# A norm applied behind its projection, and a gated attention in another order

## The reference, cut to what is touched

```python
# end of the first block, and its gated linear attention (2 pairs of heads, width 64 and 128)
x = x + 0.5 * m_l[8] * swiglu(modulate(rms_norm(x, norm3_w), m_l[6], m_l[7]), ffn2_w1, ffn2_w3, ffn2_w2)
x = rms_norm(x, final_norm_w)
# second block
xn = rmsnorm(h, norm_mix_g)
q, k, v, u, y = split(xn @ w_in, [512, 1024, 1536, 2048])
attn = dilated_mixture_attention(rope(q), rope(k), v)
uc = centred_depthwise_conv(u, conv_w, conv_b)
rec = bidirectional_rglru(uc, ...) * gelu(y)
h = h + concat([attn, rec]) @ w_out
h = h + memory_cross_attention(rmsnorm(h, norm_cross_g), rmsnorm(mem, norm_mem_g), w_cq, w_ck, w_cv, w_co)
```

## Time and profile before

| | us |
|---|---|
| median of three runs | 2144.28 |
| lowest, highest | 2143.29, 2144.73 |
| the execution that was profiled | 2144.28 |
| its span in the profile | 2142.5 |

### The profile page before, as it was taken

The page is one execution under the profiler, slowest core; times in us unless marked ns, Lnnn a source line. Parts: engine busy times, 40 slices in busy tenths (PEclk is TensorE's granted clock), DMA queues, the critical chain, the costliest instruction groups (busy, mean ns, idle before and its releaser), DMA issues.

```text
span 2142.5 us, 26436 instructions
## 1 busy us (share of the span) xinstructions
PE 2000.4 (93%) x9594; PEld 1671.9 (78%) x9594; DVE 913.5 (43%) x1361; ACT 748.5 (35%) x1056; POOL 732.9 (34%) x324
## 2 busy tenths in 40 slices
PE   5999999999989999778899999979988989999997
PEld 2999999999967775455788888857764857888886
DVE  4633377235444404773411212168976444121124
ACT  4321122112337115443342222346646344232231
POOL 1333233323413221242344443524340323443532
PEclk8999999999989999978999999989989999999999
DMA  8332244234312221001223232323140212332321
GB/s 322 120 126 75 83 160 165 78 118 148 117 45 83 60 64 43 20 1 40 93 89 116 80 108 89 109 68 108 60 128 1 89 49 80 108 99 87 108 85 63
DMA packets 53273, 197.20 MB, mean 92 GB/s; under 512 B 6304, under 2 KB 6864, under 8 KB 51408
## 3 DMA queue, kind: packets, MB, share of 16 engines
q1 hardware_dynamic: 44272, 162.98, 23.8%
q10 hardware_dynamic: 8928, 33.23, 4.3%
HBM read 194.09 MB, written 2.10 MB: 92 GB/s over the span
## 4 chain that ended last, share of the span: by engine, by line
PE 62%; issue 19%; DVE 8%; POOL 6%; ACT 3%; DMA 1%; SPq 1%; POOLq 0%; DVEq 0%; ACTq 0%
PE ps L1715 49%; POOL wlo L517 6%; PE ps L1702 1%; PE ps L1703 1%; PE ps L1704 1%; PE ps L2014 1%; DMA ada_f<-ada_p 1%; PE ps L1945 1%; PE ps L1936 1%; DVE s_gla L1434 1%; PE ps L1729 1%; PE ps L2101 1%; PE ps L2085 1%; PE ps L2075 1%; PE ps L2122 1%
## 5 line engine op out<-in xcount | busy, mean ns | idle before, releaser
L517 POOL TENSOR_TENSOR wlo<-raw,whi 128x1024 fp32r<-128x1024 f32 x280 | 692.6, 2486 | 1319.5 <-ACT whi L553 1297.5
L1715 PE MATMUL ps<-h_hi,whi 128*128 128x512 f32 (+2 forms) x1568 | 510.3, 364 | 16.5 <-POOL wlo L517 8.5
L1715 PE MATMUL ps<-h_lo,whi 128*128 128x512 f32 (+2 forms) x1568 | 507.6, 362 | 0.0
L1715 PE MATMUL ps<-h_hi,wlo 128*128 128x512 f32 (+2 forms) x1568 | 506.8, 362 | 0.0
L553 ACT ACTIVATE whi<-raw 128x1024 fp32r<-128x1024 f32 x280 | 289.5, 1053 | 417.5 <-PE ps L1715 339.5
L1715 PEld LDWEIGHTS ps<-h_hi,whi 128*128 128x128 f32 x1568 | 287.8, 189 | 57.6 <-issue 8.5
L1715 PEld LDWEIGHTS ps<-h_lo,whi 128*128 128x128 f32 x1568 | 288.3, 189 | 33.2 <-issue 1.0
L1715 PEld LDWEIGHTS ps<-h_hi,wlo 128*128 128x128 f32 x1568 | 288.2, 189 | 33.4
L1715 PE MATMUL ps<-g_hi,wlo 128*128 128x512 f32 (+1 forms) x784 | 257.3, 364 | 0.0
L1715 PE MATMUL ps<-g_hi,whi 128*128 128x512 f32 (+1 forms) x784 | 257.3, 364 | 0.0
L1715 PE MATMUL ps<-g_lo,whi 128*128 128x512 f32 (+1 forms) x784 | 257.3, 364 | 0.0
(11 more groups left out here) (385 smaller groups left out, 2304.2 us busy)
## 6 DMA issues: line engine op xcount, KB each, us to landing
raw<-panels SPq DMA_DIRECT2D x280, 512.0 KB, 3.5
ada_w<-ada_t ACTq DMA_DIRECT2D x54, 512.0 KB, 4.3
ada_f<-ada_p SPq DMA_DIRECT2D x8, 1024.0 KB, 18.7
x_lat<-x_t SPq DMA_DIRECT2D x1, 2048.0 KB, 7.9
out<-x_lat SPq DMA_DIRECT2D x8, 256.0 KB, 2.2
x_ctx<-ctx_t SPq DMA_DIRECT2D x1, 1024.0 KB, 9.9
cond_b<-cond SPq DMA_DIRECT2D x1, 1024.0 KB, 23.1
ada_x<-ada_t SPq DMA_DIRECT2D x2, 512.0 KB, 21.3
```

What stands on the lines that cost most here:

```text
L517: pool.tensor_tensor(wlo[:, sl], raw[:, sl], whi[:, sl].bitcast(f32), ALU.subtract).then_inc(lo_done, 1)
L1715: ins = pe.matmul(bank(banks + b, n), wt[:, w], a[:, at_(kc, c0):at_(kc, c0) + n], start=kc == 0 and j == 0, stop=kc == n_k - 1 and j == 2)
```

## The change

**Between the blocks.** Norm 4 becomes late. The memory's squares, their sum, the split with its weight (`memory_squares`, `memory_sums`, `memory_hi`, `memory_lo`), the sum over partitions and the root (`memory_stats`, `memory_root`, `memory_inverse`) move between the groups of the feed-forward layer. In the last group each output is scaled by the product of both weights and split (`mix_parts`, `scaled_hi`); the sums come in the middle of the first pair, the transposes behind it (`mix_spread`). 1/rms is applied later: to u and y by VectorE on their way out of PSUM (`scaled_in`), to q and k through the cosines and sines, to v and cv as ScalarE's scale, to ck by VectorE (`memory_keys`). gelu then runs in place on ScalarE. `final_rows`, the block's own norm of `x_lat`, comes behind the first two pieces. The load of `mem` starts before W_out.

**Recurrence.** `RG_STEPS` gives every step its piece; two steps of part 3 stand between the roundings for v.

**Gated attention.** The context's exponentials are made before the last fill piece, into a tile `ctx_x` of their own; VectorE's head 3 steps and ScalarE's last rounding move into the first levels; level 7's masked copy goes to ScalarE (four copies of 64 rows); and the first pair's norm product waits behind all levels of the second, with `spread_copy` taking the factors out of PSUM.

```diff
@@ input_projection2, ScalarE
+                act.wait_ge(mem_ready, 1)
+                act.wait_ge(cs_arg, 1)
...
+                    if kind == "v":
+                        for c, step in enumerate((None, 1, 2, None)):
+                            q = P_WIN2 + first + 3 + c
+                            if step:
+                                rg_step(3, step)
+                            round_panel(q % RING, q // RING + 1, q - RING)
...
+                    if n == 0:
+                        mix_root()
...
                     elif kind == "y":
+                        act.wait_ge(win2_evac, 4 + j + 1)
+                        y = ry[:, j * LAT:(j + 1) * LAT]
+                        act.activation(y, y, ACT.Gelu_apprx_tanh).then_inc(gelu_done, 1)
...
+                    if n in RG_STEPS:
+                        rg_step(*RG_STEPS[n])
@@ hidden_down, VectorE
+                def mix_parts(o):
+                    scaled_lo(norms[4], o)
+                    if o:
+                        add_both(o)
...
                         if o and G["layer"] == 1:
+                            mix_parts(o - 1)
...
+                    if G["layer"] == 1:
+                        mix_parts(KC - 1)
@@ input_projection2, VectorE
+                def scaled_in(n):
+                    dve.wait_ge(panel_done, done(P_WIN2 + n))
+                    dve.wait_ge(lat_rows, 1)
+                    dst = (ru if n < 4 else ry)[:, n % 4 * LAT:(n % 4 + 1) * LAT]
+                    dve.tensor_tensor(dst, bank(2 * (n % RING)), r_lat[:, :], ALU.mult).then_inc(win2_evac, 1)
...
+                scaled_in(0)
+                scaled_in(1)
+                final_rows()
...
+                for c in range(4):
+                    if c >= 2:
+                        scaled_in(c)
+                    rg_convolution(c)
+                dve.wait_ge(rg_conv, 4)
+                scaled_in(4)
+                scaled_in(5)
+                scaled_in(6)
...
                 rg_gated(0)
+                scaled_in(7)
...
                 rotate(6)
+                memory_keys(0)
+                memory_keys(1)
                 rotate(7)
+                memory_keys(2)
+                memory_keys(3)
@@ input_projection2, TensorE
-                first_pair(P_WIN2, (0, 2), H_BEFORE[4], token_cols(LAT))
+                pe.wait_ge(down_evac, x_final(4) + 6)
+                first_pair(P_WIN2, (0, 2), H_BEFORE[4], token_cols(LAT), late=norms[4])
+                mix_spread()
@@ retention, ScalarE
                     if j + 1 < HEADS:
                         forward_decays(j + 1)
+                    else:
+                        act.wait_ge(pv_done, 6 * HEADS)
+                        act.dma_start(masks[:, :], level_masks).then_inc(masks_loaded, 16)
+                        act.dma_start(diag2_sb[:, :], diag2).then_inc(masks_loaded, 16)
+                        context_factors(0)
                     projected(FILL[j], FILL_BANK)
```

More of the change, by code:

```diff
@@ new lines, in memory_hi, with mix_root @@
+            def memory_hi():
+                for kc in range(KC):
+                    act.activation(h_hi[:, KC * LAT + kc * CTX:KC * LAT + (kc + 1) * CTX], x_ctx[:, kc * CTX:(kc + 1) * CTX], ACT.Copy,
+                                   scale=vcol("norm_mem_g_2", kc)).then_inc(mem_hi, 1)
+            def mix_root():
+                act.wait_ge(means_ready, 1)
+                act.activation(rms[:, 0:2 * LT], rms[:, 0:2 * LT], ACT.Sqrt).then_inc(root_ready, 2)
+                act.wait_ge(rstd_ready, 4)
+                act.activation(r_lat[:, :], bank(7), ACT.Copy)
+                act.activation(r_mem[:, :], bank(5, CTX), ACT.Copy).then_inc(lat_rows, 1)
@@ L834, in gla, with spread_copy @@
                 pair_hi(1)
+            def spread_copy():
+                act.wait_ge(spread_ready, HEADS + 1)
+                for a in range(2):
+                    ins = act.activation(f_pair[a][:, :], bank(NORM_BANKS[a]), ACT.Copy)
+                ins.then_inc(pair_rows, 1)
             def context_factors(hp):
@@ L1458, in gla @@
                     scaled(0, u)
-                    if u - 1 <= MASKED:
+                    if u == 1:
+                        for t in range(1, TILES):
+                            head_norm_step(HEADS - 1, t)
+                    if u == 2:
+                        head_lo(HEADS - 1)
+                    if u - 1 < MASKED:
                         masked(0, u - 1)
@@ L1732, in first_pair @@
                             ins.then_inc(panel_done, 1)
-                    if late is not None and kc == KC // 2:
+                    if late is not None and kc == (3 if late.n == 4 else 4):
                         late_stats(late)
@@ L1738, in late_stats @@
                 pe.wait_ge(sum_done, (m.n + 1) * (KC - 1))
+                if m.n == 4:
+                    for t in range(2 * LT):
+                        src = act_a[:, t * P:(t + 1) * P] if t < LT else prod[:, TOK + (t - LT) * P:TOK + (t - LT + 1) * P]
+                        ins = pe.matmul(bank(5, 1, t), src, ones_k[:, 0:1], start=True, stop=True)
+                    ins.then_inc(stats_ready, 2)
+                    return
                 for t in range(LT):
@@ L1741, in late_stats, with mix_spread, memory_stats @@
                 ins.then_inc(stats_ready, 1)
+            def mix_spread():
+                pe.wait_ge(diag_ready, 5)
+                for b, c in ((7, LT), (3, 0)):
+                    if b == 7:
+                        pe.wait_ge(mem_inverse, 1)
+                        for t in range(2):
+                            pe.transpose(bank(5, P, t * P), mem_rms[:, t:t + 1].broadcast_to([P, P]), ident[:, :])
+                    for t in range(LT):
+                        ins = spread(bank(b, P, t * P), c + t)
+                    ins.then_inc(rstd_ready, 1)
+            def memory_stats():
+                pe.wait_ge(mem_summed, 1)
+                for t in range(2):
+                    ins = pe.matmul(bank(7, 1, t), mem_sum[:, t * P:(t + 1) * P], ones_k[:, 0:1], start=True, stop=True)
+                ins.then_inc(mem_stats, 1)
             def late_spread(m):
@@ L2188, in _ @@
                 hidden_down(G)
-            norm(norms[4])
+                if G["n"] == 1:
+                    memory_stats()
             input_projection2()
```

273 lines of the change are left out of this document (155 added, 118 removed).

## The result

The changed kernel takes 2123.81 us (median of four, 2121.73 to 2125.89), the kernel before 2144.51 beside it (median of four): a ratio of 0.9909, interval 0.9897 to 0.9921. 2116 was forecast with a range up to 2125. So the sign and the range held, but only 20.7 of the 28.4 us are there, and the forecast proper (2112 to 2120) was missed.

The account below looks back on a forecast made before the run. TensorE, busy 93% of the span, was taken as the bound, with time to win only where it waits or runs at half rate. Gains 18.4 + 3.7 + 5.4 + 1.4 less 0.5 took 2144.28 to 2116 us, range 2108 to 2125.

Parts of the forecast that it names:

- The norm between the blocks: From the last feed-forward product to panel 2: late norm starts panel 2 sooner, -18.4 us, between -14.5 and -19.9.
- I let TensorE go on at 1411.3 without a gap: Between the blocks: the first pair starts right at the last feed-forward product's end, no wait, and takes 10.8 us.
- the two need 4.54 and fall back by 0.46: Last feed-forward group: VectorE, kept from running beside GpSimd, falls behind on seven outputs, 3.2 us, mostly caught up.
- some 3 us later: Between the blocks: by the skill's VectorE and GpSimd exclusion rule, the 3.2 us queue would be lost in full.
- The gated attention: Two pairs of heads: first pair -3.7 us (bounds -1 and -5), second -5.4 (bounds -3 and -6).
- The projection: From panel 2 to the first self attention scores: ends 144.5 us after its start, -1.4, bounds -6 and +5.
- With part 3's root inside the values' panels the wait for panel 23 goes: Projection, values' panels: moving the recurrence's root there removes TensorE's 3.19 us wait.
- now the memory's last panels wait for `memory_keys`, which stands behind two rotations: Projection's end: last panels wait for VectorE's key copies; no separate price, over 5 us would prove the forecast wrong.
- (a): Rival, projection: ScalarE's in-order waits for VectorE make panels 8, 16 or the values late; price 7, 2123 us; chance 0.20.
- (d): Rival, projection: VectorE becomes the bound, with 12 evacuations stretched to 2.77 us beside GpSimd; 2149 us; chance 0.03.
- (c): Rival, gated attention: levels stay paced by GpSimd and a slow TensorE; 4 us less gain, 2120 us; chance 0.08.
- 141 to 150 us: Sign, projection: the time expected from panel 2 to the first scores of self attention if the forecast holds.

Follow-up runs that it names:

- squares_psum: Changed kernel, but ScalarE writes the squares of outputs 1 to 7 of the last feed-forward group into two free PSUM banks for VectorE's additions: 2119.9 us, ratio 0.9883.
- keys_early: Changed kernel with VectorE's first two copies of the memory's keys before rotation 6 instead of behind it: 2124.7 us, ratio 0.9912.
- round_first: Changed kernel with ScalarE's squares of the last feed-forward group one output later, behind the rounding and the next output's split: 2128.4 us, ratio 0.9924.
- changed_again: The changed kernel measured once more, unaltered: 2125.7 us, ratio 0.9920 to the kernel before.
- norm_alone: The kernel before with all of the change except its gated attention edits: 2133.8 us, ratio 0.9948.
- proj_order: Changed kernel with part 3's root behind the values' copies, rotation 5 during VectorE's wait for it, memory's keys before rotations 6 and 7: 2120.0 us, ratio 0.9878.

## Why the prediction was right or wrong

**The norm between the blocks** (-18.4 forecast, -16.1). The mechanism was right, and the step that failed is the sentence "I let TensorE go on at 1411.3 without a gap". I counted what the pair needs from the activations (6 outputs, the split of output 5) and not what it needs from the weights: the rounding is in the same ScalarE queue as the squares. From the last product: the pair 2.7 late and 1.7 long (half rate), the sums 0.2 and the transposes 0.6 shorter than put down, the wait at the sums 0 and not 1.5. That makes 18.3 of the 18.5 measured, where 16.2 was forecast. The queue that does it had been worked out ("the two need 4.54 and fall back by 0.46", 3.2 us), but I took it that most of it is caught up, and looked for the rest at the sums. squares_psum shows what this term is: without it the stage gives 20.5, beyond the bound of 19.9.

**The rule of the Trainium skill** had been put at "some 3 us later". 2.3 came, with the earlier trace rows's 2.31 as the better guide than its 0.95. That the two are near is in part luck: the 3.2 us were looked for at the sums, where nothing came, and the delay ahead of the pair is worth 4.4 by squares_psum.

**The memory's work under the feed-forward layer** was hidden from TensorE as said: 367.0 for 367.2, even the half microsecond isn't seen. What the prediction counted for ScalarE it didn't count for VectorE: the sines' arguments hold that engine for 9 us ahead of the last group.

**The gated attention** (-9.1 forecast, -10.2). To the first values' products 40.8 us for 45.6 from the last fill piece: -4.7 for -3.7. VectorE's first level starts 4.9 us sooner and the second 4.2, although TensorE did fall to half rate (0.64 in 892 to 900). 1.0 of the 4.7 is chance, since the last level's products ran faster in this execution than in keys_early, where the same part takes 41.9 us, just the -3.7:

```profile
915.47 2.00 PE L2140 MATMUL ps<-q_lv,k_lv 64*128 64x256 f32 x16 [0.39 <-DVE k_lv L1512]
```

```profile
915.44 3.03 PE L2140 MATMUL ps<-q_lv,k_lv 64*128 64x256 f32 x16 [0.19 <-DVE k_lv L1512]
```

In the second pair, from level 1 to the values, 32.2 for 36.6: -4.4 for -5.4; the last level's products took 3.79 us at half rate, for 2.83 before. And 1.7 us came from values' products at full rate in this execution, which is chance as well (last section): in keys_early and round_first, where they ran at half rate as before, the stage is 156.0, a gain of 7.4. So of the 10.2 some 2.8 are luck, and without them the stage falls short of the 9.1.

**The projection** (-1.4 forecast, +7.3; 8.5 in changed_again and norm_alone) is where the forecast failed. The early part held: panel 8 was rounded 28.7 us after panel 2's start (28 said), the values began at 92.8 (91.7 said), nothing of the wait of 3.19 is left. Two steps failed, both behind the values' start. First: "With part 3's root inside the values' panels the wait for panel 23 goes" is true, but I didn't ask what else stands behind that root; two roundings and the values' own copies do, 4.98 us for 2.15 and half rate behind it. Second: "now the memory's last panels wait for `memory_keys`, which stands behind two rotations" was written down without a price, and named again at the end as what would prove me wrong ("over 5 us"); it was 5.22. With the rows at hand (three steps of a rotation at 2.77 instead of 0.69, for two rotations) the price could have been worked out.

**The rivals.** (a) has the number (2123), the direction and the kind of cause, ScalarE waiting in its order for VectorE, but not the places: neither panel 8 nor 16 was late, the values began 1.1 later than forecast, and gelu behind the convolutions cost nothing (ScalarE waited 14.5 us for it and no one for ScalarE). The range held because it took in this price, not because the forecast's own steps came true. (d) is out: the evacuations from PSUM took 0.69 each, beside GpSimd too:

```profile
1447.33 2.40 POOL L531 TENSOR_TENSOR wlo<-raw,whi 128x1024 fp32r<-128x1024 f32 x1 [14.98 <-ACT whi L567]
1448.51 0.69 DVE L1604 TENSOR_TENSOR ry<-ps,r_lat 128x512 f32<-128x512 f32 x1 [3.61 <-PE ps L1845]
```

(c), the levels at half rate, is partly there, 1 us in the second pair. Of my own signs, "panel 2 no more than 16 us after the last product" (18.5), "141 to 150 us" (153.2) and the clock of 1.0 failed, and pointed at the right two stages.

## What to carry to other kernels

When an engine gets more work in a loop, look along the whole ring: who waits for it in order, and what unrelated work (here the rounding of weights) is queued behind that wait. A VectorE addition with both inputs in SBUF cost here the time until GpSimd was through, up to 2.88 us for 0.68; putting one input in PSUM was worth 4.4 us with nothing else changed. A sentence of the form "now X waits for Y" in a forecast needs a number at once, from the rows of Y.

## What the runs showed that I had not expected

The first four executions of the changed kernel lie at two levels, 2121.8 and 2125.8; the five of changed_again lie between 2122.8 and 2127.2 without such a gap. The stages show where they differ. The values' products of the attention follow a stretch in which TensorE is busy in short pieces. The first eight of them in the first and in the second pair, in the changed kernel, then in keys_early, then the second pair in changed_again, last the first pair before the change:

```profile
919.71 3.67 PE L2154 MATMUL ps<-s_gla,gv 128*128 128x512 f32 x8 [2.25 <-ACT s_gla L911]
...
964.74 5.37 PE L2154 MATMUL ps<-s_gla,gv 128*128 128x512 f32 x8 [2.25 <-ACT s_gla L911]
```

```profile
920.71 5.37 PE L2154 MATMUL ps<-s_gla,gv 128*128 128x512 f32 x8 [2.25 <-ACT s_gla L911]
```

```profile
964.57 3.67 PE L2154 MATMUL ps<-s_gla,gv 128*128 128x512 f32 x8 [2.25 <-ACT s_gla L911]
```

```profile
925.88 5.37 PE L2014 MATMUL ps<-s_gla,gv 128*128 128x512 f32 x8 [2.26 <-ACT s_gla L866]
```

The same instructions of the same program behind the same wait take 3.67 or 5.37 us, by the clock that they find: the granted clock of the 5.3 us from their start is 1.00 in the first pair of the changed kernel (2.4 GHz) and 0.68 in the second (1.2 GHz, then 2.4). Both at half rate, one, and none: the stage takes 156.1, 153.3 and 150.7. These products alone don't fix it: in proj_order both pairs are at half rate (5.37 and 5.27 us) and the stage is 154.6. A second such place is the norm 1 (TensorE's products there 2.15 or 3.38 us from start to the transposes' start), a third the cross attention, 1.6 us. The projection differs too: changed_again has 0.7 us less of waits than the changed kernel's first profile and 1.9 more in the products between them. Before the change both pairs were at half rate in the profiled executions of before and norm_alone (163.4, 163.6). So an edit of 4 us, as in keys_early, can be lost in the median of four and stand clear in its stage. What decides which level an execution gets, these runs don't show.
